# A fifth buffer for second expert weights, loads no longer held for the gathers, and filler matmuls, in a one-core block with a routed expert layer

## What is computed

```python
h = rmsnorm(x, norm1_g) * (1.0 + scale1) + shift1
mix, new_lru, new_gla = mixer(h, ...)        # input product, recurrence, linear attention, output product
x = x + gate1 * mix
h = rmsnorm(x, norm2_g) * (1.0 + scale2) + shift2
x = x + gate2 * hier_moe(h, ...)             # below
y = rmsnorm(x, final_g)

# hier_moe: 4 groups of 4 experts; each row takes one group and the two best experts in it
hid = jnp.einsum('nd,edf->nef', xt, exp_w13)            # exp_w13: 16 x 1024 x 512
a, bgl = jnp.split(hid, 2, axis=-1)
act = jax.nn.silu(a) * bgl * gate[:, :, None]
out = jnp.einsum('nef,efd->nd', act, exp_w2)            # exp_w2: 16 x 256 x 1024
```

## Time and profile before

| | |
|---|---|
| median of three runs | 571.24 us (571.23 to 571.52) |
| the profiled execution | 571.2 us |
| its span, first to last instruction | 569.4 us |
| TensorE busy | 514.4 us (90%) |
| VectorE, ScalarE, GpSimd busy | 288.1, 193.3, 89.1 us |
| mean granted TensorE clock | 0.968 of full speed |
| moved by DMA | 120.53 MB |

### The profile page before, as it was taken

The page is one execution under the profiler, slowest core; times in us unless marked ns, Lnnn a source line. Parts: engine busy times, 40 slices in busy tenths (PEclk is TensorE's granted clock), DMA queues, the critical chain, the costliest instruction groups (busy, mean ns, idle before and its releaser), DMA issues.

```text
span 569.4 us, 7601 instructions
## 1 busy us (share of the span) xinstructions
PE 514.4 (90%) x2906; PEld 258.1 (45%) x2906; DVE 288.1 (51%) x629; ACT 193.3 (34%) x356; POOL 89.1 (16%) x101
## 2 busy tenths in 40 slices
PE   3899999999999999999999999929999999949970
PEld 2445545554444566566545555524344443313320
DVE  4522655949410674212245545575766665735571
ACT  6322289991502220345312212111000345430531
POOL 3000000000420220000000000022033345522333
PEclk9999999999999999999999999958999999988995
DMA  8997655115471930810006580579899999998611
GB/s 321 387 270 230 189 176 194 37 34 175 168 288 38 345 118 2 243 37 1 1 0 222 181 335 24 199 257 338 325 362 396 393 382 374 387 372 310 234 55 66
DMA packets 72567, 120.53 MB, mean 212 GB/s; under 512 B 12033, under 2 KB 29778, under 8 KB 72530
## 3 DMA queue, kind: packets, MB, share of 16 engines
q1 hardware_dynamic: 63896, 104.23, 52.5%
q0 software_dynamic: 8496, 15.75, 7.7%
q10 hardware_dynamic: 138, 0.04, 0.0%
HBM read 112.36 MB, written 22.84 MB: 237 GB/s over the span
## 4 chain that ended last, share of the span: by engine, by line
PE 53%; DMA 6%; DVE 3%; ACT 2%; issue 1%; SPq 0%; POOL 0%; POOLq 0%; ACTq 0%; DVEq 0%
PE ps L1471 12%; PE ps L1184 11%; PE ms L1562 10%; PE ms L1558 5%; DMA wring<-in_exp_w_dram 4%; PE ps L1593 4%; PE ps L1589 2%; PE ps L1535 2%; PE ms L1444 1%; DMA mixT<-h_rows,slot_tok 1%; DMA sg<-in_state_gla_dram 1%; PE ps L1411 1%; PE ps L1401 1%; PE ps L1354 1%; PE ps L1435 1%
## 5 line engine op out<-in xcount | busy, mean ns | idle before, releaser
L1184 PE MATMUL ps<-r,wring 128*128 128x512 f32 (+1 forms) x512 | 143.5, 437 | 1.5 <-ACT mixT L972 0.9
L1184 PEld LDWEIGHTS ps<-r,wring 128*128 128x128 f32 x512 | 78.9, 191 | 67.2 <-issue 66.9
L1471 PE MATMUL ps<-wring,mixT 128*128 128x512 f32 x160 | 72.3, 598 | 0.3 <-DVE mixT L1956 0.3
L1562 PE MATMUL ms<-wring,tmp 128*32 128x512 f32 x288 | 67.8, 605 | 0.0
L749 POOL DMA_INDIRECT mixT<-h_rows,slot_tok x13 | 16.5, 1270 | 181.7 <-DVE slot_tok L2118 172.0
L1471 PEld LDWEIGHTS ps<-wring,mixT 128*128 128x128 f32 x160 | 29.2, 190 | 31.2 <-issue 31.2
L1258 PE MATMUL ps<-wring,r 128*128 128x512 f32 x80 | 35.6, 598 | 0.5 <-issue 0.5
L1118 ACT ACTIVATE tmp<-ms 128x256 f32<-128x256 f32 x13 | 5.0, 383 | 85.9 <-PE ms L1562 57.6
L1593 PE MATMUL ps<-wring,gd 128*32 128x512 f32 x144 | 32.5, 592 | 0.0
L1562 PE MATMUL ms<-r,tmp 128*32 128x512 f32 x144 | 24.4, 659 | 8.4 <-DMA wring<-in_exp_w_dram 8.4
L1091 ACT ACTIVATE gd<-xres 128x512 f32<-128x512 f32 x10 | 6.3, 630 | 56.7 <-DVE xres L1995 56.7
(11 more groups left out here) (366 smaller groups left out, 814.9 us busy)
## 6 DMA issues: line engine op xcount, KB each, us to landing
wring<-in_ada_w_dram SPq DMA_DIRECT2D x12, 2048.0 KB, 11.2
wring<-in_exp_w_dram SPq DMA_DIRECT2D x7, 2048.0 KB, 19.8
wring<-in_exp_w_dram SPq DMA_DIRECT2D x10, 1024.0 KB, 9.2
wring<-in_w_in_dram SPq DMA_DIRECT2D x16, 512.0 KB, 5.0
r<-in_exp_w_dram SPq DMA_DIRECT2D x4, 2048.0 KB, 16.1
tmp<-in_exp_w_dram SPq DMA_DIRECT2D x4, 2048.0 KB, 17.9
wring<-in_w_out_dram SPq DMA_DIRECT2D x2, 2048.0 KB, 11.9
vtok<-in_exp_w_dram SPq DMA_DIRECT2D x4, 1024.0 KB, 16.7
```

The lines of the kernel that those rows point to most:

```text
L1184: i = mm(d, lhsT, r, start=first, stop=last)
L1471: i = mm(product(f"mx{t}")[:, half * 512:(half + 1) * 512], mixT[:, k, t * P:(t + 1) * P], w[:, k, :], start=(k == 0), stop=(k == KD - 1))
L1562: i = mm(ms[r:r + 32, b, :], xgT[:, b, k, r:r + 32], w[:, k, :], start=(k == 0), stop=(k == KD - 1), skip_group_check=True)
```

## The change

Four edits; the rest of the kernel, the load order and the order on VectorE, ScalarE and POOL are as they were.

1. `e2` gets a fifth buffer, of two pieces that lie apart (`qk[:, 0:D]` and `mtmp`). So that a buffer may lie in pieces, every `load2` becomes two transfers of 512 KB, one for each k. The second weights have a slot list (`load2_slot`) and a release list (`freed2_by`) of their own. `load2(4)` waits for nothing but the expert's number, and `load2(n)` follows `load13(n)` from n = 5.
2. SP no longer waits for the first gather before loads 3: `load2(3)` comes right behind the last half of `e13` load 2, and `load13(3)` after the stores of `h2` have landed.
3. `fing` moves to a free part of `r1` and is loaded at the end of the attention.
4. `keep_going(n)` issues n matmuls of 128x384 into a PSUM bank that is free: three after `router(4)`, six after the last `table`.

```diff
-        e2 = [w.rearrange("p (k f) -> p k f", k=DC) for w in e2]
+        e2 = [[w[:, k * D:(k + 1) * D] for k in range(DC)] for w in e2] + [[qk[:, 0:D], mtmp]]
...
-        fing = tmp[:, 4 * N:4 * N + D]
+        fing = r1[:, W_WORDS:W_WORDS + D]
...
         load_slot = [0, 1, 2, 3, 0, 2, 1, 3, 0, 2, 1, 3, 0, 1, 2, 3]
         freed_by = [None] * 4 + [0, 1, 2, 2, 3, 4, 5, 6, 7, 8, 9, 9]
+        load2_slot = [0, 1, 2, 3, 4, 0, 2, 1, 3, 4, 0, 2, 1, 3, 0, 4]
+        freed2_by = [None] * 5 + [0, 1, 2, 2, 3, 4, 5, 6, 7, 8, 9]
...
             wait_taken(sp, f"oT{NT - 1}")
             for kind in range(4):
                 load_row(1, kind)
+            sp.dma_start(fing, final_g.rearrange("(a n) -> a n", a=1).to_broadcast([P, D])).then_inc(fg_in, 16)
...
             def load2(n, e):
                 w = exp_w2[0, bass.ds(e, 1)].rearrange("a (k p) f -> p (a k) f", p=P)
-                sp.dma_start(e2[load_slot[n]], w).then_inc(e2_in[load_slot[n]], 16)
+                for k in range(DC):
+                    sp.dma_start(e2[load2_slot[n]][k], w[:, k, :]).then_inc(e2_in[load2_slot[n]], 16)
...
-            sp.wait_ge(gx_in[0], 16)
+            load2(3, first[3])
             sp.wait_ge(logits_ready, NT)
             for i in range(2):
                 sp.wait_ge(h2_out[i], 16 * ((NT - i + 1) // 2))
             load13(3, first[3])
-            load2(3, first[3])
-            sp.wait_ge(h2_ready, NT)
-            sp.dma_start(fing, final_g.rearrange("(a n) -> a n", a=1).to_broadcast([P, D])).then_inc(fg_in, 16)
             sp.wait_ge(ordered, 2)
-            before_it = None
-            for n in range(4, NE + 1):
-                if n < NE:
-                    e = expert_of(n)
-                    sp.wait_ge(hid, freed_by[n] + 1)
-                    load13(n, e)
+            for n in range(4, NE):
+                e = expert_of(n)
+                if n == 4:
+                    load2(n, e)
+                sp.wait_ge(hid, freed_by[n] + 1)
+                load13(n, e)
                 if n > 4:
-                    sp.wait_ge(y_done, 2 * (freed_by[n - 1] + 1))
-                    load2(n - 1, before_it)
-                before_it = e
+                    sp.wait_ge(y_done, 2 * (freed2_by[n] + 1))
+                    load2(n, e)
...
             router(NT - 1, 1)
+
+            def keep_going(n):
+
+                for _ in range(n):
+                    mm(ps[:, 2, 0:3 * P], ident[:, :], sg0[:, 0:3, :].rearrange("p g v -> p (g v)"), start=True, stop=True,
+                       skip_group_check=True)
+
+            keep_going(3)
             rank(NT - 1)
...
             table(NT - 1)
+            keep_going(6)
...
+            def second_weights(n):
+                return 16 * DC * load2_slot[:n + 1].count(load2_slot[n])
```

## The result

The changed kernel takes 573.8 us (median of 9 runs, 572.39 to 575.79) against 570.6 us for the kernel before on the same chip (570.09 to 571.59). The ratio is 1.0046 [1.0031, 1.0061]: slower by some 2.6 us, where 2.0 was forecast. A second series gave 1.0038 [1.0014, 1.0061]. A difference between two kernels' times is from the ratios unless I say otherwise.

A forecast was written before the change was run, and what follows sets the result against it. TensorE bounds the stage, waiting for gather 0 and, through queued transfers, load 13. Gather +2.9, chain before it -0.5, block 0 -0.4, all else 0 give +2.0 on 571.2: 573.2 us, range 568.6 to 575.8 (forecast's own 571.5 to 575).

The forecast's parts named there:

- the late gather: Before block 0: gather 0 meets loads 3, takes about 7.5 us, and lands 2.9 us later (bounds 0 and 4.2).
- Loads 3 not held: At the stage's start: loads 3 go out at about 374 to 376, delaying gather 0 by 2.9 us; TensorE gains nothing.
- The turn-taking rival: Gather 0 and loads 3 take turns on the DMA engines: gather 1.4 us late, 571.7 us in all; chance 0.07.
- the one with the gather behind all of loads 3: Loads 3 go first: gather 4.2 us later, block 0 loses 0.6 more, 575.5 us; chance 0.12.
- The fifth buffer and the order of the loads: SP queue ahead of load 13: still nine first and eight second weights, so the 8.4 us wait shortens by 0.
- the final weights: Their 0.52 MB leave the queue at 386 for about 301: worth 0, up to 1.4 us without the 405 to 410 slack.
- The clock: Fillers before `rank` and gather 0 gain 0.5 us on the chain and 0.4 in block 0 (ends +2.05 and -0.6).
- the rise 3.5 to 4.1 us after work resumes: TensorE's clock rises this long after work resumes, so three fillers from 371.8 bring it back at about 375.5.
- Halved transfers: Each second weight in two transfers instead of one, ahead of load 13: cost 0, ends 0 to 0.8 us.
- The estimate of 16 us: Eight more transfers before load 13 at a fixed 2.0 us each, if none overlapped: 16 us longer.
- the signs that I named: Gather 0 about 7.5 us, ending near 387; load 13 wait about 8 us; clock 1.0 in 376 to 386; DMA share near 1.

The follow-up runs named there:

- second profile: Profile of the changed kernel run again without edits, in a second series against the kernel before: ratio 1.0038, median 574.53 us, gather 0 7.9 us.
- not held only: Kernel before without the wait of loads 3 for gather 0, nothing else: ratio 1.0046 to the kernel before, median 574.54 us.
- first profile: Profile of the changed kernel's fastest run of the first nine: span 570.6 us, before 569.4; that series' ratio to the kernel before was 1.0046.
- held: Changed kernel with the wait of loads 3 for gather 0 put back: ratio 1.0011 to the kernel before, median 572.38 us.
- fillers only: Kernel before with the nine filler matmuls and nothing else: ratio 0.9988 to the kernel before, median 571.22 us.
- lagged: Changed kernel with second weight n - 1 instead of n behind first weight n: ratio 1.0040 to the kernel before, median 573.1 us.
- held and lagged: Changed kernel with loads 3 waiting for gather 0 again and second weight n - 1 behind first weight n: ratio 0.9975 to the kernel before, 570.41 us.
- fillers in the wait: The held and lagged kernel with eight more filler matmuls before the first half of `hidden(10)`: ratio 0.9908 to the kernel before, median 567.49 us.

## Why the prediction was right, and where not

The sign and the main term, the late gather, were right, and the range held: 2.0 us forecast, 2.6 measured. That the sum came out so near is partly luck. The gather cost 2.7 to 3.5 us where I had 2.9. In the second profile, whose time is the median of its series, the fillers and the clock came out 2.6 us dearer than I had them (1.7 lost instead of 0.9 won), and 1.5 less up to the end of the wait made up for part of it. Neither profile shows a sum of 2.0: from the end of `mx4` on, the first is 0.1 us longer than before and the second 4.7.

*Loads 3 not held.* Right, and shown: the wait removed alone gives 1.0046, put back it gives most of it back. Gather 0 took 7.3 to 8.1 us in the five profiles without the hold and 4.5 to 4.7 in all others; the forecast was 7.5. The turn-taking rival, 1.4 us late, was too low, and the one with the gather behind all of loads 3 (8.8 us) nearer, though neither fits.

*The fifth buffer and the order of the loads.* The result of 0 for the wait was the wrong step. The count of nine and eight loads from 406.86 on is right, but it leaves out second weight 4, which no longer stands among them and is moved all the same: behind loads 3 there are now nine second weights ahead of load 13 (4 to 12), not eight (4 to 11). It would have been free only if the DMA engines had had room for all of it before the queue builds up. With loads 3 held they had room for about half (share 0.89 in the 13 us from 404.97), and the fifth buffer alone cost 1.5 us up to the end of the wait. For the final weights I had relied on the same room; without them the wait was 1.3 us shorter, near the end of 1.4 that I had given. With loads 3 early, that stretch has room (0.73). The early loads alone gave 0.8 us back at load 13 (7.6 instead of 8.4, not held only); with the other edits it is 1.0 and 1.5 us (7.4 and 6.9), and no run parts what the early loads and the final weights give there. I had said that nothing comes off the queue. That term was off by 1.0 to 1.5 us, in the direction of a faster kernel.

*The clock.* It was the other mis-sized term, and in the second profile it went the other way. I had block 0 gaining 0.4 and the chain before it 0.5. In the first profile they gave 1.5 and 0.4, in the second they cost 0.8 and 0.9: the rise 3.5 to 4.1 us after work resumes, read from two places, failed there (383.4 instead of 375). The second profile is the exception in front of the gather: in the other seven with fillers gather 0 is issued 11.8 to 12.1 us behind `mx4`, before 12.50, so the 0.5 for this part was right as a rule. In block 0 I had the six fillers at full clock and done early, and a gain of 0.4. Four profiles went that way (held, fillers only, lagged, held and lagged): the clock was lost in block 0, and it gained nothing, 10.1 to 10.3 us from `turn_x(0)` to `turn_x(1)` with 10.1 before. The 1.5 us of the first profile came another way: there the six ran mostly at half clock and ended later, and the clock was kept. The six fillers in the profile of held loads and in the first profile after:

```profile
376.98 4.12 PE L1523 MATMUL ps<-sg,ident 128*128 128x384 f32 x12
378.60 6.75 PE L1522 MATMUL ps<-sg,ident 128*128 128x384 f32 x12
```

Of the seven profiles with six fillers before gather 0, block 0 kept the clock in two, the first after and fillers in the wait, both with slow fillers (6.75 and 6.73 us). The break between the fillers and `turn_x(0)` does not part the cases: 3.0 us in both of the profiles shown. I left out that a shorter wait at load 13 is partly paid back: 5.77 and 6.52 us behind it instead of 5.39. Over the profiles without fillers in it, a wait of 8.3 to 8.9 us was followed by 5.2 to 6.1 us, one of 6.8 to 7.6 by 5.8 to 6.5.

*Halved transfers.* Zero was right: 0.9991 [0.9977, 1.0005]. The estimate of 16 us rested on the fixed 2.0 us for each transfer of the Trainium skill (DMA: Bandwidth & Descriptors, Anatomy of one DMA — SWDGE (gpsimd) path). The page measured it for transfers issued from GpSimd, and these are issued from SP and queue behind each other; here no such cost shows.

*Of the signs that I named,* the gather and its end at 387 to 388 came, as did a DMA share of 1.00 from 379.5 to 382. The clock at 1.0 from 376 to 386 did not come: it was 0.50 for much of that time in both profiles.

What stays open: why the runs of the changed kernel and of the fifth buffer alone spread over 3.4 to 5.5 us and those of held and lagged over 1.6. The kernel before spread over 1.5 us in the first series and over 3.4 to 3.5 in the others, so the spread is not only the change's. The mean clock differs between runs of the changed kernel (0.968 in the slowest of the first nine, 0.977 in the fastest), and two profiles show it lost at block 0 in one and not in the other; no run here takes it as the only cause. Open is also why the clock fell where it did. The fifth buffer's 2.0 us are nearly accounted for in its profile: 0.5 less up to `turn_x(1)`, 1.5 more to the end of the wait and 0.7 more behind it are 1.6 (its 64 matmuls of block 0 took 7.55 us, before 8.13).

## What to carry to other kernels

A transfer that the critical path waits for should not share the DMA engines with bulk loads that nobody needs yet: the hold was worth about 2.6 us in the kernel before and 1.5 to 2.0 in the changed one, although it left the engines idle. Whether another buffer or an early load helps depended here on whether the DMA engines had idle time between it and the transfer that is waited for: where they had, its bytes did not lengthen that wait (with the early loads alone it was 0.8 us shorter); where they had not, it lengthened that wait, and taking bytes out from in front of it shortened it. A wait that cannot be removed can be used to keep TensorE's clock up: going by their times it worked in all but one run of each of the two kernels that did it.

## What the runs showed of the hardware

An indirect gather of 128 rows of 4 KB took 4.5 to 4.7 us (nine profiles) with no bulk load queued and 7.3 to 8.1 us (five profiles) with 3 MB issued up to 6 us ahead. Sixteen loads of 1 MB in a row of loads, each cut into two of 512 KB, cost nothing that eleven runs can tell (0.9991). Keeping TensorE busy through a wait of about 7 us ahead of one block took 32 matmuls from 6.52 to 3.64 us in one profile and left them at 6.60 in another. Fillers did not always bring the clock back: once 14.9 us of work in 16.6 us went by at a mean clock of 0.59.
